# The second scan's merge is multiplied inside its groups and its tail

## The reference, cut to what matters

```python
gate_ssm, gate_gdn = sigmoid(h @ w_g_ssm), sigmoid(h @ w_g_gdn)        # 1024 wide
merged = gate_ssm * (y_ssm @ w_ssm_up) + gate_gdn * (y_gdn @ w_gdn_up) # y: 2048 wide
x = x + mod * rmsnorm(merged @ w_out)                                   # then the MLP
```

## Time and profile before

| | us |
|---|---|
| device time, three runs | 3784.92 median (3783.27 to 3789.3) |
| profiled execution, span | 3787.3 |
| TensorE busy in it | 3436.4 (91%) |
| VectorE / ScalarE / GpSimd busy | 2168.0 (57%) / 1266.0 (33%) / 1075.5 (28%) |
| mean granted clock of TensorE | 0.94 |

### The profile page before, as it was taken

One profiled execution on the slowest core, in us unless ns is written; L12 is line 12 of the kernel. 1 busy time (PEld: TensorE's weight loads), 2 busy tenths in 40 slices (PEclk: granted clock), 3 DMA queues, 4 the chain that ended last, 5 costly groups with the idle time before them and its releaser, 6 DMA issues. The chain is left out here.

```text
span 3787.3 us, 57179 instructions
## 1 busy us (share of the span) xinstructions
PE 3436.4 (91%) x22384; PEld 2913.5 (77%) x22384; DVE 2168.0 (57%) x3179; ACT 1266.0 (33%) x1980; POOL 1075.5 (28%) x458
## 2 busy tenths in 40 slices
PE   6987998999998979899989998999999988969998
PEld 4767887888887768688868887778787776757886
DVE  5668535564565585454476887335666664345334
ACT  4135423122122254332234444323433342233222
POOL 3210013322222210344423332432232222424442
PEclk8979999999998889899989999999999998989998
DMA  5430012332333500233312221221111111213231
GB/s 180 159 112 2 1 45 73 106 117 89 106 107 129 169 19 1 84 128 117 111 65 73 66 66 50 89 73 50 40 40 46 34 35 50 84 50 101 95 98 58
DMA packets 85328, 295.26 MB, mean 78 GB/s; under 512 B 13506, under 2 KB 14082, under 8 KB 84740
## 3 DMA queue, kind: packets, MB, share of 16 engines
q1 hardware_dynamic: 84836, 290.74, 23.7%
q10 hardware_dynamic: 288, 1.60, 0.1%
HBM read 290.21 MB, written 2.10 MB: 77 GB/s over the span
## 5 line engine op out<-in xcount | busy, mean ns | idle before, releaser
L275 POOL TENSOR_TENSOR mlp_slab_lo<-slab,mlp_slab_hi 128x1024 fp32r<-128x1024 f32 x144 | 363.2, 2526 | 483.3 <-ACT mlp_slab_hi L256 483.3
L275 POOL TENSOR_TENSOR slab_kept_lo<-slab,slab_kept_hi 128x1024 fp32r<-128x1024 f32 x99 | 244.2, 2467 | 728.6 <-ACT slab_kept_hi L256 728.6
L2079 DVE TENSOR_TENSOR mlp_hid_lo<-mlp_sq,mlp_hid_hi 128x512 fp32r<-128x512 f32 (+1 forms) x96 | 213.5, 2224 | 120.8 <-ACT mlp_hid_hi L2035 120.3
L149 PE MATMUL banks<-mlp_hid_hi,mlp_slab_hi 128*128 128x512 f32 (+1 forms) x768 | 279.6, 364 | 0.0
L150 PE MATMUL banks<-mlp_hid_lo,mlp_slab_hi 128*128 128x512 f32 (+1 forms) x768 | 278.8, 363 | 0.0
L151 PE MATMUL banks<-mlp_hid_hi,mlp_slab_lo 128*128 128x512 f32 (+1 forms) x768 | 278.6, 363 | 0.0
L256 ACT ACTIVATE mlp_slab_hi<-slab 128x1024 fp32r<-128x1024 f32 x144 | 151.6, 1056 | 375.9 <-PE banks L151 325.9
L150 PE MATMUL banks<-hT_mlp_lo,mlp_slab_hi 128*128 128x512 f32 (+1 forms) x576 | 205.2, 356 | 0.0
L149 PE MATMUL banks<-hT_mlp_hi,mlp_slab_hi 128*128 128x512 f32 (+1 forms) x576 | 205.0, 356 | 0.0
L151 PE MATMUL banks<-hT_mlp_hi,mlp_slab_lo 128*128 128x512 f32 (+1 forms) x576 | 204.7, 355 | 0.0
L2076 DVE TENSOR_TENSOR mlp_sq<-mlp_tmp 128x512 f32<-128x512 f32 (+1 forms) x96 | 101.2, 1054 | 178.4 <-ACT mlp_tmp L2030 178.4
(11 more groups left out here) (597 smaller groups left out, 9497.4 us busy)
## 6 DMA issues: line engine op xcount, KB each, us to landing
slab<-in_s_mlp_dram SPq DMA_DIRECT2D x192, 512.0 KB, 3.7
proj_vec_slab<-in_s_vec_proj_dram SPq DMA_DIRECT2D x64, 512.0 KB, 3.7
mlp_vec_slab<-in_s_vec_mlp_dram SPq DMA_DIRECT2D x64, 512.0 KB, 3.6
slab<-in_s_ssm_dram SPq DMA_DIRECT2D x48, 512.0 KB, 3.5
slab<-in_s_gdn_dram SPq DMA_DIRECT2D x48, 512.0 KB, 3.6
slab<-in_s_in_dram SPq DMA_DIRECT2D x32, 512.0 KB, 4.7
slab<-in_s_out_dram SPq DMA_DIRECT2D x24, 512.0 KB, 4.4
slab<-in_s_merge_ssm_dram SPq DMA_DIRECT2D x24, 512.0 KB, 3.5
```

Source lines behind the costliest of these rows:

```text
L149: nc.tensor.matmul(out, lhs.hi, rhs.hi, start=start, stop=False)
L275: self.nc.gpsimd.tensor_tensor(pair.lo[:], self.raw[u % slots][:], pair.hi[:].bitcast(F32), ALU.subtract).then_inc(self.split, 1)
L2079: nc.vector.tensor_tensor(hid.lo[:, u, :], sq[:, u % 2, :], hid.hi[:, u, :].bitcast(F32), ALU.subtract).then_inc(hid_ready, 1)
```

## The change

The merge of the second scan is gone as a stage. A `ScanPlan` gives one order of 72 slabs. In groups i = 1 to 7 a "middle" and a "late" slab are added: gates 0 to 3 in groups 1 and 2, then up slabs, each with the rows of one quarter of the scan's output (two groups) and two output columns of 128 ("o" 0 and 1, four k steps each). Two more up slabs and gates 4 to 7 go into the last group, the last quarter's four up slabs into the last group and the tail. Per level the middle slab gives one k step after the first half's W products and the rest at the top level; the late slab stands before the transposes. `steps` puts 28 z steps between the chunks. The up products are summed in `c.xl` (x is stored to memory at the stage's start and loaded back in `post_product`); gates wait in spare tiles. Outputs leave the transposes as a high half by ScalarE (`place`) and a low half by VectorE (`low`). The decay masks are made by ScalarE (`logs`: eight copies of 128 x 128 with a scale). The loops of ScalarE, GpSimd and VectorE are unrolled.

```diff
+        self.last = [("up", 3, b) for b in range(4)]
...
+        for i in range(GROUPS):
+            first, second, z = ([("u", i, j) for j in (0, 1)], [("u", i, j) for j in (2, 3)], [("z", i, j) for j in (0, 1)])
+            slabs = first + some(early, i) + second + some(middle, i) + z
+            self.order += slabs + some(late, i)
...
+        self.order += tail + self.last
+        self.turns += [x for x in blocks(tail + self.last) if x not in apart]
+        self.apart = apart
+        self.slab = {x: n for n, x in enumerate(self.order)}
+        self.turn = {x: n for n, x in enumerate(self.turns)}
+        self.moved = {x: n for n, x in enumerate(blocks(moved))}
+        self.ups = {x: n for n, x in enumerate(y for y in self.order if y[0] == "up")}
+        gates = [x for x in tail if x[0] == "gate"]
...
+    def extra(self, pe, x, k0=0, k1=KT):
+
...
+        if k0 == 0:
+            c.ring.slab(pe, 0, n)
+        for k in range(k0, k1):
+            o, kt = (k // 4, k % 4) if up else (0, k)
+            if kt == 0:
+                self.wait_bank(pe, x, o)
+            if up and kt % 2 == 0:
+                pe.wait_ge(self.low_made, 4 * x[1] + kt + 3)
+            src = self.pair[:, (4 * x[1] + kt) % 8, :] if up else c.hT[:, k, :]
+            last = product3(nc, self.out(x, o), w[:, k * P:(k + 1) * P], src, kt == 0, kt == (3 if up else KT - 1))
+            if up and k == 3:
+                last.then_inc(self.half_full, 1)
+            elif k == KT - 1:
+                last.then_inc(freed, 1)
+
+    def full(self, eng, x, o=0):
...
+    def move(self, dve, x, o=0):
+
...
+        self.full(dve, x, o)
+        if x[0] == "gate":
+            nc.vector.tensor_copy(self.gates(x[1]), self.out(x)).then_inc(self.moved, 1)
+            return
+        out = self.total[:, 2 * x[2] + o, :]
+        if x[1] == 0:
+            nc.vector.tensor_copy(out, self.out(x, o)).then_inc(self.moved, 1)
+        else:
+            dve.wait_ge(self.moved, self.plan.moved[("up", x[1] - 1, x[2]), o] + 2)
+            nc.vector.tensor_tensor(out, out, self.out(x, o), ALU.add).then_inc(self.moved, 1)
...
+    def rounds(self, act, x):
+
+        n = self.plan.slab[x] + 3 if x else SCAN_SLABS
+        if n < SCAN_SLABS:
+            self.c.ring.round_slab(act, 0, n)
...
+        for j in range(2):
+            n = (2 * g + j) % 8
+            dve.wait_ge(self.placed, 2 * g + j + 2)
+            self.c.nc.vector.scalar_tensor_tensor(out=self.pair.lo[:, n, :], in0=self.c.ps[:, j, :], scalar=self.weight(2 * g + j),
+                                                  in1=self.pair.hi[:, n, :].bitcast(F32), op0=ALU.mult, op1=ALU.subtract).then_inc(self.low_made, 1)
...
-        steps = [0, 2, 3, 4, 6, 7, 8, 10, 11, 12, 14, 15, 16]
+        steps = [0, 2, 4, 7, 9, 11, 14, 16, 18, 21, 23, 25, 28]
...
+                sp.dma_start(saved_x, c.xl[:]).then_inc(saved, 16)
...
+                        if hf == 0 and lev:
+                            m.extra(pe, x, lev - 1, lev)
+                    if top:
+                        m.extra(pe, x, lev, KT)
...
+                    if i < GROUPS:
+                        m.z(pe, i, steps[n], steps[n + 1])
+                    elif n < 8:
+                        m.extra(pe, ("gate", 7), n, n + 1)
+                    else:
+                        k = (0, 1, 4, 5)[n - 8]
+                        m.extra(pe, plan.last[0], k, k + 1)
...
                         pe.wait_ge(am_ready, g + 2)
+                        for n in range(2):
+                            if (plan.late.get(g), n) in plan.moved:
+                                pe.wait_ge(m.moved, plan.moved[plan.late[g], n] + 2)
...
+                        pe.wait_ge(low_made, g * 2 + 1)
...
-                        z(i, 16, 32)
+                        if i < GROUPS:
+                            m.z(pe, i, 28, 32)
+                            m.extra(pe, plan.late[i])
+                        else:
+                            for k in (0, 4):
+                                m.extra(pe, plan.last[1], k, k + 2)
+                            pe.wait_ge(o_ready, g * 4 + 5)
+                            for k in (0, 4):
+                                m.extra(pe, plan.last[2], k, k + 2)
...
+                m.extra(pe, plan.tail[0])
+                m.extra(pe, plan.tail[1])
+                scan(GROUPS - 1, 0, GROUPS)
+                m.extra(pe, ("gate", 4))
+                scan(GROUPS - 1, 1, GROUPS)
+                m.extra(pe, ("gate", 5))
+                for part in (2, 4, 5):
+                    scan(GROUPS - 1, part, GROUPS)
+                for x in plan.last[:3]:
+                    m.extra(pe, x, 2, 4)
+                    m.extra(pe, x, 6, 8)
+                m.extra(pe, plan.last[3])
...
+                def logs(g):
+                    for ch in range(T4):
+                        for h in range(2):
+                            n = SSM_H + 2 * g + h
+                            last = nc.scalar.activation(am[:, ch, h, :], c.upto, ACT.Copy, scale=c.rates[:, R_LOG, ch, n:n + 1])
+                    last.then_inc(am_ready, 1)
```

ScalarE's program for one group (unrolled), GpSimd's and VectorE's:

```diff
+                    act.wait_ge(yt_full, g * 2 + 1)
+                    for j in range(2):
+                        silu(g, j)
+                        act.wait_ge(sil_ready, g * 4 + j + 2)
+                        nc.scalar.activation(sq[:, j, :], sil[:, j, :], ACT.Square).then_inc(qk_sq, 1)
+                    if more:
+                        take(i, 0)
+                        m.rounds(act, ("u", i, 0))
+                    else:
+                        m.rounds(act, plan.tail[0])
+                        m.rounds(act, plan.tail[1])
+                    for b in range(2):
+                        act.wait_ge(dec_full, g * 2 + b + 2)
+                        nc.scalar.activation(dec[:, 2 * b:2 * b + 2].rearrange("p t h f -> p (t h f)"), c.ps[:, 2 + b, :], ACT.Exp).then_inc(dec_ready, 1)
+                    silu(g, 2)
+                    silu(g, 3)
+                    for j in range(2):
+                        act.wait_ge(sums, g * 2 + j + 2)
+
+                        nc.scalar.activation(roots[:, j, :], c.ps[:, j, 0:T4], ACT.Sqrt, bias=c.eps if j else c.eps_k,
+                                             scale=1.0 if j else float(P)).then_inc(qk_root, 1)
+                    if more:
+                        take(i, 1)
+                        m.rounds(act, ("u", i, 1))
+                    else:
+                        m.gate_out(act, 4)
+                        m.rounds(act, ("gate", 4))
+                    for b in range(2):
+                        act.wait_ge(v_turned, g * 2 + b + 2)
+                        for ch in (2 * b, 2 * b + 1):
+                            last = nc.scalar.activation(vtok[:, ch, :], c.ps[:, b, (ch % 2) * 256:(ch % 2) * 256 + 256], ACT.Copy, scale=roots[:, 1, ch:ch + 1])
+                        last.then_inc(vtok_ready, 1)
+                    act.wait_ge(k_turned, g + 2)
+                    nc.scalar.activation(ktok[:].rearrange("p t f -> p (t f)"), c.ps[:, 4, :], ACT.Copy).then_inc(ktok_ready, 1)
+                    if more:
+                        take(i, 2)
+                        m.rounds(act, ("u", i, 2))
+                        take(i, 3)
+                    else:
+                        m.gate_out(act, 5)
+                    level(g, 1)
+                    m.rounds(act, ("u", i, 3) if more else ("gate", 5))
+                    for lev in range(2, LEVELS):
+                        level(g, lev)
+                    if more:
+                        m.rounds(act, plan.middle[i])
+                    else:
+                        m.gate_out(act, 6)
+                        m.rounds(act, ("gate", 6))
+                        m.gate_out(act, 7)
+                        m.rounds(act, ("gate", 7))
+                        for b in range(4):
+                            m.gate_in_place(act, b)
+                        nc.scalar.activation(warm[:], c.eps, ACT.Sqrt)
+                    act.wait_ge(o_ready, g * 4 + 5)
+                    act.wait_ge(w_ready, g * 12 + 13)
+                    nc.scalar.activation(flat(o_sq_), flat(o), ACT.Square).then_inc(o_sq, 1)
+                    if more:
+                        logs(g + 1)
+                    act.wait_ge(gated, g + 2)
+                    nc.scalar.activation(stat[:, 1, :], stat[:, 0, :], ACT.Sqrt, bias=c.eps, scale=1.0 / P).then_inc(root, 1)
+                    if more:
+                        take(i, 4)
+                        m.rounds(act, ("z", i, 0))
+                        take(i, 5)
+                        m.rounds(act, ("z", i, 1))
+                    m.place(act, g, yt_full)
+                    if more:
+                        m.rounds(act, plan.late[i])
 
                 act.wait_ge(zeroed, 2)
-                run_groups(act, takes, scan, ring)
+                logs(0)
+                for n in range(3):
+                    ring.round_slab(act, 0, n)
```

(50 more changed lines are left out.)

333 lines of the change are left out of this document (212 added, 121 removed).

## The result

| | before | after |
|---|---|---|
| device time, median (range) of four runs each | 3784.1 us (3783.14 to 3789.3) | 3754.3 us (3753.1 to 3756.5) |
| span of the profiled execution | 3787.3 | 3751.2 |
| ratio, 95% interval | | 0.9919, [0.9905, 0.9933] |

The change makes the kernel 29.8 us faster, not 50.5. The time lies inside the range on record.

The account below looks back on a forecast made before the run. TensorE's own work plus gaps and slow-clock stretches was taken as the bound. First interval 117 + 6 x 86.6 + last group 86.5 + tail 32.6 = 755.7 against 806.2 us; 50.5 off 3784.92 gives 3734.4 us, range 3700 to 3766.

Parts of the forecast that it names:

- the late first slab: Group start: the next group's first slab is rounded behind the first z take, so TensorE waits 2.7 us.
- the group's head: Group start on VectorE: late convolutions and splits holding up the masks cost 5.3 us an interval, bounds 0 and 8.
- 1.2 us before level 0 and 0.6 more before level 1: Before the levels: middle and z splits hold up VectorE's chain from `roots` to mask 0, so TensorE waits this long.
- The convolutions end 3.5 us later, and so do `roots` and the turns that wait for them: Group start: VectorE's moves, low halves and one more split cost 3.5 us, containing TensorE's 2.7 us slab wait.
- The tail: After the last group: VectorE's sums end it, 32.6 us in place of the 153.0 us merge, bounds 24 and 40.
- +0.3 us a level: Levels 1 to 5: three inserted matmuls (0.68 us) mostly fill gaps, adding 0.3 us each, 1.5 in all.
- lets in its nine matmuls for about 0.3: Top level: some 2 us of waits take in nine middle-slab matmuls (2.04 us) for about 0.3 us.
- gate-branch (z) products respaced, +1.0: Among the four chunks: twelve more z products cost 1.6 us, less some slow-clock time regained: +1.0 us an interval.
- The late slab: From last chunk to transposes: a slab replaces most z products while transposes still wait for VectorE: +0.1 us.
- The slow clock follows each new wait: After each new 2.7 us slab wait: TensorE's clock drops, up to 12 us unless VectorE's lateness covers it, 3746; chance 0.16.
- Last group: Last group of the second scan: like the other intervals, with inserted products and extra moves, 86.5 us for 72.7 before.
- four more moves on VectorE between its convolutions: Last group: four moves take 2.8 us of VectorE's time, of which 2 us were counted.

Follow-up runs that it names:

- experiment 1: Changed kernel, but ScalarE rounds the next group's first slab before waiting for the last chunk's output rows: 3739.3 us, ratio 0.9873.
- experiments 2: Changed kernel, but GpSimd splits the middle slab after mask 1 and the first z slab after mask 3: 3744.9 us, ratio 0.9889.
- experiment 6: Changed kernel, but VectorE again makes the decay masks, ahead of the convolution, instead of ScalarE: 3763.5 us, ratio 0.9946.
- 10: Experiment 1's kernel, with GpSimd splitting only 64 of most slabs' 1024 columns, so the output is not the reference's: 3703.1 us, ratio 0.9784.
- experiment 5: Changed kernel, but TensorE multiplies the middle slab as one block before the levels, not spread over them: 3747.4 us, ratio 0.9903.
- experiment 3: Changed kernel, but VectorE copies chunk 0's value rows to `R` before the levels, not after: 3748.8 us, ratio 0.9898.
- experiment 4: Changed kernel, but VectorE's moves in the last group come after convolution columns 0 and 2, not 1 and 3: 3753.2 us, ratio 0.9910.
- kernel 11: Changed kernel with earlier first-slab rounding, roots first, middle slab as block, z split, `R` copy, first masks and last-group moves shifted, another bank: 3710.1 us, ratio 0.9806.
- experiment 9: Kernel before the change, with only the second scan's group loops on VectorE, GpSimd and ScalarE unrolled: 3785.6 us, ratio 1.000.
- experiment 8: Changed kernel with the edits of experiments 1 to 4 together and ScalarE's first masks behind its first rounded slab: 3732.0 us, ratio 0.9855.

## Why the prediction was right and where it was wrong

**Right: the late first slab, and the size of the group's head.** "It waits 2.7 us": 2.48 to 2.81 in the seven groups, for the cause named. "1.2 us before level 0 and 0.6 more before level 1": 0.63 (1.13 in two of six) and 0.63. From the transposes to the top level, the levels' own increase left out, the interval from 2907.31 has 5.1 us more than that of before, where the sum has 5.3.

**Not right about what sets the turns.** "The convolutions end 3.5 us later, and so do `roots` and the turns that wait for them": VectorE's convolutions and the roots are 2.7 later, and the turns, 3.7 later, wait for neither. The sum took VectorE's lateness to contain TensorE's; in four of six intervals it was the other way round, with the slow clock on top. Only one of the six has a wait for `roots`. That experiment 1 brings this wait back, and that experiments 2, 6, 10 show the splits holding VectorE, makes VectorE the next bound, close behind.

**The tail: 32.4 for 32.6, by luck in its parts.** VectorE's last add,

```profile
3288.56 1.28 DVE L3206 TENSOR_TENSOR mT<-mT,xl 128x512 f32<-128x512 f32 x2
```

ends 22.7 us after the tail's first product (3267.14), as in the sum, and the output product follows 6.8 later (6.7). But VectorE's operations start 0.60 us apart, not 0.72, the two splits hold it 2.7 us, not 4, and it starts 1.5 later and waits 2.35 more for TensorE's products, which run at a granted clock of 0.75 over the tail. The errors cancel.

**Wrong: "+0.3 us a level" and "lets in its nine matmuls for about 0.3".** The levels cost +0.58 each and the top +1.8 (4.76 for 2.96): 4.7 where the sum has 1.8. I had taken 0.46 us between the half sets as free, and named 0.2 more at the level's start that the +0.3 doesn't use (with it the sum would be +0.1). Only the recorded 0.25 was free; the triple starts 0.61 us after the half set, so the rest is time that the half set takes itself. And the top level's "some 2 us of such waits" were 1.1 (0.36, 0.54 and 0.18, in the trace of before as in experiment 5). Experiment 5 confirms it: without the triples a level is 3.49 us again and the top 2.96, and as a block the same 24 matmuls cost no more. This is the largest single error, 2.9 us an interval at the full clock, some 20 us in seven groups.

**Missing: the copy to `R`.** The sum gives nothing to chunk 0's own copy. It reads and writes SBUF, the late slab's split now falls on it, and TensorE waits 1.11 to 1.16 us in the first group and the six intervals (experiment 3). The Trainium skill (SBUF — State Buffer, "SBUF: two separate sides") has a VectorE operation in a two-port mode, or with two SBUF inputs, shut out for the whole of a running GpSimd instruction. The trace agrees for both kinds: this copy 2.35 us against 0.29, the `dec` products 3.60 against 1.43, and no change for an operation with one input in PSUM. My sentence on this page had only the case of two SBUF inputs; the copy has one, so by the page it is the other case (the trace doesn't show the mode). I had applied the rule to the masks and not gone through the rest of VectorE's list with it.

**Over-priced: "gate-branch (z) products respaced, +1.0".** From the first z product behind the top level to the start of the last chunk's last product it is 18.94 us in the interval from 2907.31. Without chunk 0's wait for `R` that is 17.8. Before it was 18.43 in the interval from 2718.54, where the clock fell in this place, and 17.10 in that from 2952.59, where it didn't. So at the full clock the twelve z products cost 0.7 us for their 4.3, and the slow clock that is no longer here gave back 1.3 (1.4 was expected): -0.7, where the sum has +1.0. The late slab, "+0.1", is -0.2. In the interval compared this gave back 1.9 of the 4 us of the two errors above.

**"The slow clock follows each new wait" was partly true.** Behind the slab wait the granted clock is 0.88 over 14 us, and two slabs take 12.6 us for 11.0, in four of six intervals. In the second and the sixth it stays at 1.00 over the same stretch, after waits of 2.81 and 2.58. That prices it within one kernel: the second interval, at 1.00 throughout, is 87.46 us, its neighbours with the slow clock 88.05 to 88.16. The slow clock takes 1.4 us of TensorE's time there and costs the interval 0.6 to 0.7, because the wait for mask 0 behind it shrinks from 1.1 to 0.6, as the rival's own condition said. That is some 2.6 of the 9.6 us by which the path's six intervals exceed the forecast.

**Last group, "86.5": 91.4.** The step "four more moves on VectorE between its convolutions" counts them as VectorE's time. They are also what frees the bank of the second tail slab:

```profile
3187.85 0.62 PE L151 MATMUL banks<-gdn_rows_hi,slab_kept_hi 128*128 128x512 f32 x1 [4.02 <-issue]
```

The profile names no releaser for these 4.02 us. VectorE's two moves of the first tail slab begin at 3187.07, and moving them earlier (experiment 4) changed the wait to 2.92; in kernel 11, with moves earlier and another bank, it is 0.93. That it was this bank is shown; that it is worth 4 us in the whole time is not.

**In sum**, the path lost 16.0 of the 50.5 us: 9.6 in six intervals, 4.9 in the last group, 1.75 in the first, -0.2 in the tail. The other 4.7 lies in which executions are compared: I took a path from a profiled execution that is 5.2 us above its kernel's median as if it were the median's, and it is set against one that is 1.2 below (6.3 in all, less the 1.6 by which the rest of the program is shorter). One place is in the trace: the first of before's six intervals is 81.55 us at a granted clock of 0.94, the others 76.8 to 78.2, and in experiment 9 the six are 77.8 on average.

**Open:** experiment 4's missing gain, and why single intervals of the same program run at a clock of 0.96 and others at 1.00 with the same waits (kernel 11, and the changed kernel behind its slab wait). What the store of x costs by itself was not tried.

## What to carry to other kernels

Count a gap between two sets of matmuls as free only as far as the trace records a wait in it: here 0.25 of 0.46 us was, and work put in the rest pushed the chain. When GpSimd makes SBUF-to-SBUF splits, go through VectorE's whole list for operations between SBUF tiles and give each a place without a split: moving one split or one copy alone can bring the next pair together, as experiment 8 shows. And ask first whether the inserted block covers another engine's lateness as a whole before it is cut up.

## What was not expected of the hardware

- A running split of 2.4 us delays even a small copy by its whole rest: 128 x 256 took 2.35 us instead of 0.29, and 128 x 16 took 2.29 instead of 0.16 in one interval of experiment 6. Two products took 2.38 instead of 1.29. A copy that started 0.05 us before its split took 0.28 (experiment 5).
- With the slab waits gone the granted clock was 1.00 over six intervals (516 us, mean). With a wait of 2.6 us per interval it was 0.98, and 0.88 in the 14 us behind four of six such waits; behind the other two, 2.81 and 2.58 us long, it was 1.00.
- A triple of fp32r matmuls between fp32 sets costs 0.83 us (0.58 that the level grew and the 0.25 of wait that it filled) where it streams at 0.68.
- ScalarE's eight copies of 128 x 128 with a scale took 2.44 us, 0.305 each (0.30 predicted from 64 and 1024 elements).
- Loops with register addresses on three engines cost nothing measurable against unrolled ones (ratio 1.000, within 0.1%).
